# Products with V of query tile 1 issued in pairs, in the attention of a two-block kernel

## The chip, the cores and the metric

The kernel runs on one core of one Trainium2 chip. The metric is the device time of one execution in microseconds (us), as the median of several runs. Beside it stands one profiled execution, whose span runs from the first to the last instruction that the profiler recorded.

The engines are named as in the profile: PE is TensorE (matmuls), PEld its loading of weights, DVE is VectorE, ACT is ScalarE, POOL is GpSimd, SP is SyncE. L1892 is line 1892 of the kernel.

## The reference, cut to what matters

Two transformer-like blocks are computed for 256 tokens of width 1024. The first block has one projection `h @ w_in` that feeds a gated recurrence (RG-LRU) and a sparse attention with three branches: compressed keys, selected blocks of keys, and a window. With 256 tokens the selected blocks and the window both cover every key that the causal mask allows, so both branches are causal attention, each with its own K and V. The change touches the last line of this sum only in the order in which its terms are added:

```python
o_cmp = jnp.einsum('bgrqc,bgcd->bgrqd', p_cmp, v_cmp)
...
o_slc = jnp.einsum('bgrqm,bgqmd->bgrqd', p, vg)
...
o_win = jnp.einsum('bgrqk,bgkd->bgrqd', pw, vwb)
return gb[..., 0:1] * o_cmp + gb[..., 1:2] * o_slc + gb[..., 2:3] * o_win
```

There are 16 query heads in 4 groups of 4; a group shares its keys and values. After it come the output projections, a feed-forward part, and the second block.

## The kernel before

**Chunks.** All weights are streamed in the order of a list, `CHUNKS`. A chunk is up to 128x2048 numbers. For most chunks ACT rounds the weights to a high part `WH` (L629), DVE subtracts to get the low part `WL` (L1074), and PE multiplies both with the activations (L1735, L1736 and L1740 in this stretch of the kernel; a chunk of kind `rnn` has 126 columns, one of kind `mg` 128). Chunks of kind `ri` are not split; PE takes them at L2065, L2073 and L2075.

**Windows.** From chunk `W0` on, chunk W0+w is also window w. PE's program is one loop over the chunks: first the scores of a unit (if one is due), then the chunk itself, then `window(w)`.

**Units.** The attention over selected blocks and window is cut into 12 units, u = 0 to 11, three for each head group g. u%3 = 0 is query tile 0 (queries 0 to 127) with both branches at once; u%3 = 1 is query tile 1 with the first branch, and u%3 = 2 is query tile 1 with the second. A unit goes through these steps, and `UNIT_WINDOWS` says in which window w its scores stand:

- window w, ahead of the chunk: PE computes the scores, `unit_qk` (L1858). It waits for `exp_done`, that is until ACT has read the scores of unit u-1, since there is one place for scores, banks 2 and 3 of PSUM.
- DVE adds the mask (L1095) and finds the maxima (L1097), ACT takes the exponentials (`unit_exp`, L650) into `SM`, or `SMC` where u%3 = 1, and DVE multiplies by gate and reciprocal of the sum (L1112).
- window w+2, behind the chunk: PE transposes the weights, `unit_t` (L1869); ACT (L662) and DVE (L1119) copy the result to `PT`, which has two buffers, `PT[:, u % 2]`. The copy for unit u waits for `pv_done` of unit u-2, which read the same buffer.
- window w+3, behind the chunk: PE multiplies with V, `unit_pv`. For u%3 = 0 and 1 it first starts a sum in bank 6 or 7 with the compressed branch (L1884). Then come four matmuls (L1892), 64 output rows each, in alternating halves of the array. The sum of query tile 1 is left open by u%3 = 1 and closed by u%3 = 2.
- after u%3 = 0 and 2, ACT and DVE copy the sum out of the bank (`o_first` L668, `o_second` L1168) to `CHL`, which the output projection reads.

The windows of the units' scores are 5, 7, 9, 10, 11, 12, 14, 15, 16, 17, 19 and 20. The kinds of the chunks of windows 9 to 24 are mg, rnn, rnn, mg, ri, mg, rnn, rnn, mg, ri, rnn, rnn, mg, mg, ri, ao.

ACT and DVE have fixed programs too, each a loop over the chunks. In them, beside the units, stand the splits of the weights, the reading of the chunks' results, and the recurrence (ACT L717 to L727, with three loads of activation tables of 1.28 us around the square root and the gelu).

In the profile one f32 matmul of `unit_qk` or `unit_pv` counts as two instructions, so a unit's four at L1892 stand as x8.

Of the kernel before, what the change touches and what calls it, by code (L numbers as in the profile page):

```python
# [189 lines left out]
def unit_of(u):  # L190

    g, n = divmod(u, 3)
    return g, int(n > 0), max(n - 1, 0)


def unit_at(w):

    return UNIT_WINDOWS.index(w) if w in UNIT_WINDOWS else None
# [46 lines left out]
def two_block_program(nc, A_w, A_x, A_cols, A_consts, A_g1, A_g2, A_og, A_gln, A_ln1, A_ln2, A_ws, A_out):  # L245
    ctx = ExitStack()
    with ctx:
# [41 lines left out]
        def col(name, j=0, n=1, parts=P):  # L289
            lo = COLS[name][0] + j  # L290
            return CV[0:parts, lo:lo + n]
# [1422 lines left out]
        def _(eng):  # L1714
# [147 lines left out]
            def unit_t(u):  # L1862
                eng.wait_ge(p_ready, u + 1)
                if u >= 1:
                    eng.wait_ge(pt0_copied, u)
                    eng.wait_ge(pt1_copied, u)
                for part in range(2):
                    for i in range(4):
                        last = eng.transpose(PS[:, 4 + part, P * i:P * i + P], sm(u)[:, i, P * part:P * part + P], ident)  # L1869
                last.then_inc(t_done, 1)  # L1870

            def unit_pv(u):
                g, qt, br = unit_of(u)
                v = 2 * g + qt
                bank = 6 + v % 2
                if br == 0:
                    if v == 0:
                        eng.wait_ge(pct_copied, 1)
                        eng.wait_ge(vb_ready, 2)
                    if v >= 2:  # L1880
                        eng.wait_ge(o_lo, v - 1)
                    for pp in range(2):
                        j = 2 * (g % 2) + pp
                        eng.matmul(PS[:, bank, P * pp:P * pp + P],  # L1884
                                   VB[:, g // 2, 2 * j:2 * j + 2, :].rearrange("p h d -> p (h d)"),
                                   PC[:, g // 2, P * qt:P * qt + P], start=(pp == 0), stop=False, skip_group_check=True)
                eng.wait_ge(pt0_copied, u + 1)
                eng.wait_ge(pt1_copied, u + 1)
                for part in range(2):
                    key_tile, branch = (part, br) if qt else (0, part)  # L1890
                    for b in range(2):
                        last = eng.matmul(PS[64 * b:64 * b + 64, bank, 0:256], V[:, key_tile, branch, HD * g:HD * g + HD],  # L1892
                                          PT[:, u % 2, part, 2 * b:2 * b + 2, :].rearrange("p r q -> p (r q)"),
                                          start=False, stop=(part == 1 and (br == 1 or not qt)), skip_group_check=True)
                last.then_inc(pv_done, 1)

            def window(w):
                if w == 0:
                    eng.wait_ge(hg_ready, 2)
                    eng.matmul(PS[:, 3, P:P + NKV * CP], HG[:, 1, :], JJ[:, :], start=True, stop=True).then_inc(hgt_done, 1)  # L1900
                    eng.wait_ge(hk_ready, 1)
                    eng.wait_ge(hk_zero, 1)
                    eng.wait_ge(qkt_copied, 1)
                    eng.matmul(PS[0:NKV * CP, 4, 0:HD], HK[:, 0, :, :].rearrange("p g c -> p (g c)"), col("w2k", n=HD),
                               start=True, stop=True).then_inc(kc_done, 1)
                if w == 1:
                    eng.wait_ge(hvx_ready, 1)
                    eng.wait_ge(hk_zero, 2)
                    eng.wait_ge(qkt_copied, 2)
                    for T in range(2):  # L1910
                        eng.matmul(PS[:, 7, 64 * T:64 * T + 64], HVX[:, 8 * T:8 * T + 8, :].rearrange("p h c -> p (h c)"),
                                   col("w2v", n=HD), start=True, stop=True).then_inc(kc_done, 1)
                if w == 1:
                    eng.wait_ge(knc_ready, 1)
                    eng.transpose(PS[:, 5, 0:NKV * CP], KNC[:, :, :].rearrange("p a d -> p (a d)"),
                                  ident[0:NKV * CP, 0:NKV * CP]).then_inc(kct_done, 1)
                if w == 2:
                    eng.wait_ge(kcz_ready, 1)
                    for j in range(KD):
                        rows = slice(32 * (j % 4), 32 * (j % 4) + 32)  # L1920
                        last = eng.matmul(PS[rows, 5, TOK * (j // 4):TOK * (j // 4) + TOK],
                                          KCZ[:, j // 2, :, :].rearrange("p a c -> p (a c)"), QT[:, j, :], start=True, stop=True)
                    last.then_inc(sc_done, 1)
                    eng.wait_ge(knc_ready, 1)
                    for t in range(NT):
                        last = eng.transpose(PS[:, 4, TOK + 64 * t:TOK + 64 * t + 64], GTT[:, P * t:P * t + P],
                                             ident[0:64, 0:64])
                    last.then_inc(gate_t_done, 1)
                if w == 3:
                    eng.wait_ge(kcz_ready, 2)  # L1930
                    for tt in range(NT):
                        for jj in range(2):
                            o = TOK * tt + P * jj
                            last = eng.transpose(PS[:, 5, o:o + P], SCT[:, TOK * jj + P * tt:TOK * jj + P * tt + P], ident)
                    last.then_inc(sc_done, 1)
                if w == 6:
                    eng.wait_ge(pc_ready, 1)
                    for T in range(2):
                        for tt in range(NT):
                            last = eng.transpose(PS[:, 6, 256 * T + P * tt:256 * T + P * tt + P],  # L1940
                                                 SC[:, tt, 8 * T:8 * T + 8, :].rearrange("p h c -> p (h c)"), ident)
                    last.then_inc(pct_done, 1)
                u = unit_at(w - 2)
                if u is not None:
                    unit_t(u)
                u = unit_at(w - 3)
                if u is not None:
                    unit_pv(u)

            def unit2_qk(u):  # L1950
# [392 lines left out]
            for c in range(NCH):  # L2343
                u = unit_at(c - W0)
                if u is not None:
                    unit_qk(u)
                main(c)
                after(c)
                if c >= W0:
                    window(c - W0)  # L2350
# [170 lines left out]
```

## Time and profile before

| | before |
|---|---|
| median of 3 runs | 812.32 us (812.21 to 812.46) |
| span of the profiled execution | 810.6 us |
| PE busy | 799.6 us (99%) |
| DVE busy | 599.4 us (74%) |
| ACT busy | 487.0 us (60%) |
| mean granted TensorE clock | 0.998 of full |
| DMA | 143.79 MB, mean 177 GB/s |

The profiled execution is 1.7 us shorter by its span than the median run. That is what lies around the span (start and end of the program), and it is taken as the same for both kernels. The units run from about 101 us (first scores) to about 243 us (last product with V).

A row of the timeline gives start, duration, engine, line, operation, tiles, shape and count; in brackets stands the idle time before it and what ended that. Durations overlap, since a matmul starts before the one ahead has drained; what counts on the path is the distance from one start to the next.

### The profile page before, as it was taken

Reading aid. Unit: us, or ns where it says so; the run is one execution under the profiler, and the core shown is the slowest. Engines: PE = TensorE matmul, PEld = TensorE weight load, DVE = VectorE, ACT = ScalarE, POOL = GpSimd, SP = SyncE. Lnnn points to the kernel's source line nnn. Section 1 sums busy time; section 2 is a strip of 40 time slices with the busy share of each in tenths; the row PEclk is TensorE's granted clock in tenths of the full one; section 3 lists DMA queues with packets and bytes.
Section 4 is the critical chain, followed back from the end, with each engine's and each line's share of the span. In section 5 each row is a group of like instructions: output and inputs, shape, how many; then the busy total and the mean of one; then the engine's idle time right before and its main releaser. Section 6 shows DMA issues by size and latency. Waiting matters only on the chain.

```text
span 810.6 us, 11913 instructions
## 1 busy us (share of the span) xinstructions
PE 799.6 (99%) x4813; PEld 693.2 (86%) x4813; DVE 599.4 (74%) x773; ACT 487.0 (60%) x738; POOL 27.1 (3%) x38
## 2 busy tenths in 40 slices
PE   8999999999999999999999999999999999999996
PEld 7889998888888888988888888888888988888885
DVE  6774698998957986897878778877777665655556
ACT  6555598877757454765666566546755654544552
POOL 1102000000000000000000000020110000000000
PEclk9999999999999999999999999999999999999999
DMA  8446432342434674456455555764453655555441
GB/s 337 164 156 251 170 126 104 118 155 73 151 119 159 229 288 156 156 188 227 160 206 174 201 197 175 256 237 147 146 196 121 211 201 196 174 219 191 161 152 52
DMA packets 22630, 143.79 MB, mean 177 GB/s; under 512 B 2608, under 2 KB 3248, under 8 KB 8240
## 3 DMA queue, kind: packets, MB, share of 16 engines
q1 hardware_dynamic: 20880, 137.72, 48.3%
q10 hardware_dynamic: 1696, 5.31, 1.8%
q8 instruction: 38, 0.62, 0.3%
q14 instruction: 16, 0.13, 0.0%
HBM read 141.97 MB, written 1.05 MB: 176 GB/s over the span
## 4 chain that ended last, share of the span: by engine, by line
PE 93%; ACT 3%; DVE 2%; DMA 1%; issue 1%; DVEq 0%; SPq 0%; ACTq 0%
PE PS L1748 19%; PE PS L1752 10%; PE PS L1801 10%; PE PS L1802 10%; PE PS L1805 10%; PE PS L1735 5%; PE PS L1736 4%; PE PS L1740 4%; PE PS L2115 3%; PE PS L1764 2%; PE PS L2094 2%; PE PS L1858 1%; PE PS L1892 1%; PE PS L2119 1%; PE PS L1869 1%; PE PS L2065 1%
## 5 line engine op out<-in xcount | busy, mean ns | idle before, releaser
L1074 DVE TENSOR_TENSOR WL<-RAW,WH 128x2048 fp32r<-128x2048 f32 (+2 forms) x127 | 285.1, 2247 | 31.1 <-ACT WH L629 31.0
L629 ACT ACTIVATE WH<-RAW 128x2048 fp32r<-128x2048 f32 (+2 forms) x127 | 238.2, 1877 | 47.0 <-PE PS L1805 25.7
L1490 DVE TENSOR_TENSOR HLS<-PS,HLS 128x512 f32<-128x512 f32 x46 | 31.7, 689 | 92.7 <-ACT HLS L977 92.7
L1748 PE MATMUL PS<-CHL,WH 128*128 128x512 f32 x352 | 87.9, 392 | 0.0
L1735 PE MATMUL PS<-BHL,WH 128*126 128x256 f32 (+1 forms) x336 | 83.6, 287 | 0.0
L977 ACT ACTIVATE HLS<-PS 128x512 f32<-128x512 f32 x46 | 27.4, 595 | 90.7 <-PE PS L1752 86.3
L1736 PE MATMUL PS<-BHL,WH 128*126 128x256 f32 (+1 forms) x336 | 81.8, 282 | 0.0
L1748 PE MATMUL PS<-BHL,WH 128*128 128x512 f32 x320 | 79.9, 392 | 0.0
L1748 PEld LDWEIGHTS PS<-CHL,WH 128*128 128x128 f32 x352 | 63.9, 189 | 11.8
L1802 PE MATMUL PS<-WH,AHL 128*128 128x512 f32 x176 | 68.8, 391 | 0.0
L1801 PE MATMUL PS<-WH,AHL 128*128 128x512 f32 x176 | 68.7, 390 | 0.0
L1735 PEld LDWEIGHTS PS<-BHL,WH 128*126 128x126 f32 (+1 forms) x336 | 63.4, 189 | 4.6 <-issue 3.7
L1748 PEld LDWEIGHTS PS<-BHL,WH 128*128 128x128 f32 x320 | 58.1, 189 | 10.7
L1736 PEld LDWEIGHTS PS<-BHL,WH 128*126 128x126 f32 (+1 forms) x336 | 63.5, 189 | 0.0
L1801 PE MATMUL PS<-WH,BHL 128*128 128x512 f32 x160 | 63.2, 395 | 0.0
L1802 PE MATMUL PS<-WH,BHL 128*128 128x512 f32 x160 | 62.3, 390 | 0.0
L1805 PE MATMUL PS<-WL,AHL 128*128 128x512 f32 x176 | 54.4, 390 | 0.0
L1752 PEld LDWEIGHTS PS<-CHL,WL 128*128 128x128 f32 x352 | 48.0, 190 | 3.4
L1752 PE MATMUL PS<-CHL,WL 128*128 128x256 f32 x352 | 49.1, 282 | 0.0
L1740 PE MATMUL PS<-BHL,WL 128*126 128x256 f32 (+1 forms) x336 | 46.7, 281 | 0.0
L1752 PEld LDWEIGHTS PS<-BHL,WL 128*128 128x128 f32 x320 | 43.7, 190 | 3.1
L1501 DVE SCALAR_TENSOR_TENSOR CG<-HLS,CV,CG 128x255 f32<-128x255 f32 (+1 forms) x96 | 44.2, 481 | 1.7
(313 smaller groups left out, 1311.1 us busy)
## 6 DMA issues: line engine op xcount, KB each, us to landing
RAW<-in_w_stream SPq DMA_DIRECT2D x108, 1024.0 KB, 4.8
RAW<-in_w_stream SPq DMA_DIRECT2D x11, 1008.0 KB, 4.9
RAW<-in_w_stream SPq DMA_DIRECT2D x8, 704.0 KB, 4.5
WF<-in_w_stream SPq DMA_DIRECT2D x2, 1024.0 KB, 5.4
LN<-in_ln ACTq DMA_DIRECT2D x2, 1024.0 KB, 5.2
WF<-in_w_stream SPq DMA_DIRECT2D x4, 294.0 KB, 3.6
X<-in_x SPq DMA_DIRECT2D x2, 512.0 KB, 4.2
RAW<-in_w_stream SPq DMA_DIRECT2D x2, 512.0 KB, 6.8
```

Of the source, the lines that this page charges most:

```text
L629: eng.activation(WH[:, c % NSLOT, 0:CHUNKS[c][2]], raw(c), ACT.Copy).then_inc(w_hi, 1)
L1074: eng.tensor_tensor(WL[:, c % NSLOT, 0:CHUNKS[c][2]], raw(c), f32(WH[:, c % NSLOT, 0:CHUNKS[c][2]]), ALU.subtract).then_inc(w_lo, 1)
L1490: eng.tensor_tensor(HLS[:, n % 4, :, :], PS[:, bank:bank + 2, 0:TOK], HLS[:, n % 4, :, :], ALU.add)\
L1501: ins = eng.scalar_tensor_tensor(o, HLS[:, i % 4, v, 0:TOK - s], col("fw", (2 - s) * 2 * N_UP + f), o, ALU.mult, ALU.add)
L1735: eng.matmul(out, wh, H[0:parts, k, :], start=(k == 0), stop=False)
L1736: eng.matmul(out, wh, L[0:parts, k, :], start=False, stop=False)
L1740: last = eng.matmul(out, wl, H[0:parts, k, :], start=False, stop=(k == nk - 1))
L1748: eng.matmul(PS[:, bank, :], wh, HL[:, k, :, :].rearrange("p a t -> p (a t)"), start=(k == 0), stop=False)
L1752: last = eng.matmul(PS[:, bank, 0:TOK], wl, HL[:, k, 0, :], start=False, stop=(k == KD - 1))
L1801: eng.matmul(out, H[:, k, tile], wh, start=(start and n == 0), stop=False)
L1802: eng.matmul(out, L[:, k, tile], wh, start=False, stop=False)
L1805: last = eng.matmul(out, H[:, k, tile], WL[:, s, lo_:lo_ + cols], start=False, stop=(stop and n == len(ks) - 1))
```

## The change

Behind the transposes of a window, the kernel before issues the products with V of one unit. The new one leaves them out where u%3 = 1, and issues them one unit later, directly ahead of those of u%3 = 2.

```diff
                 u = unit_at(w - 3)
-                if u is not None:
+                if u is not None and u % 3 != 1:
+                    if u % 3 == 2:
+                        unit_pv(u - 1)
                     unit_pv(u)
```

So `unit_pv(1)` moves from the end of window 10 to the end of window 12, `unit_pv(4)` from 14 to 15, `unit_pv(7)` from 18 to 19, and `unit_pv(10)` from 22 to 23. The order of the units among each other stays, and with it the counts of `pv_done`. ACT's, DVE's, POOL's and SP's instructions stand in the same order as before. Nothing is added or removed.

PE around units 1 and 2, before: the end of window 10 (chunk `rnn`), window 11 with unit 2's transposes at its end, and the end of window 12 with unit 3's. L1858 are the scores of units 4 and 5, L2065 is the `ri` chunk of window 13.

```order
L1740 MATMUL PS<-BHL,WL 126x256 x8
L1884 MATMUL PS<-PC,VB 128x128 x2
L1892 MATMUL PS<-PT,V 64x256 x4
L1858 MATMUL PS<-KT,QT 128x256 x4
...
L1740 MATMUL PS<-BHL,WL 126x256 x8
L1869 MATMUL PS<-CN,SM 128x128 x8
L1858 MATMUL PS<-KT,QT 128x256 x4
...
L1740 MATMUL PS<-BHL,WL 128x256 x8
L1869 MATMUL PS<-CN,SM 128x128 x8
L1892 MATMUL PS<-PT,V 64x256 x4
L2065 MATMUL PS<-XC,WF 126x256 x4
```

The same place in the new kernel, whose lines from 1950 on stand two higher (L2067 is L2065 of before).

```order
L1740 MATMUL PS<-BHL,WL 126x256 x8
L1858 MATMUL PS<-KT,QT 128x256 x4
...
L1740 MATMUL PS<-BHL,WL 126x256 x8
L1869 MATMUL PS<-CN,SM 128x128 x8
L1858 MATMUL PS<-KT,QT 128x256 x4
...
L1740 MATMUL PS<-BHL,WL 128x256 x8
L1869 MATMUL PS<-CN,SM 128x128 x8
L1884 MATMUL PS<-PC,VB 128x128 x2
L1892 MATMUL PS<-PT,V 64x256 x8
L2067 MATMUL PS<-XC,WF 126x256 x4
```

Unit 1's six matmuls have moved past the scores of units 4 and 5, two chunks and two groups of transposes.

PE around units 4 and 5, before: the end of window 14 (chunk `mg`) with unit 5's transposes, and the end of window 15 (chunk `rnn`). L1858 are the scores of units 7 and 8.

```order
L1869 MATMUL PS<-CN,SM 128x128 x8
L1884 MATMUL PS<-PC,VB 128x128 x2
L1892 MATMUL PS<-PT,V 64x256 x4
L1858 MATMUL PS<-KT,QT 128x256 x4
...
L1740 MATMUL PS<-BHL,WL 126x256 x8
L1892 MATMUL PS<-PT,V 64x256 x4
L1858 MATMUL PS<-KT,QT 128x256 x4
```

The same place in the new kernel.

```order
L1869 MATMUL PS<-CN,SM 128x128 x8
L1858 MATMUL PS<-KT,QT 128x256 x4
...
L1740 MATMUL PS<-BHL,WL 126x256 x8
L1884 MATMUL PS<-PC,VB 128x128 x2
L1892 MATMUL PS<-PT,V 64x256 x8
L1858 MATMUL PS<-KT,QT 128x256 x4
```

Here unit 4's matmuls have moved past one group of scores and one chunk. Units 7 and 10 move likewise past one chunk; unit 10's past an `ri` chunk, and no scores.

## Rows read from the trace of the kernel before

**Rows 1.** The page, part 1: busy time, share of the span, instructions of each engine.
```profile
PE 799.6 (99%) x4813; PEld 693.2 (86%) x4813; DVE 599.4 (74%) x773; ACT 487.0 (60%) x738; POOL 27.1 (3%) x38
```

**Rows 2.** Waits of PE, whole span: line, waited for, us in total, times, longest.
```profile
PE PS L2335 <- ACT XN L1026: 1.4, 1, 1.4
PE PS L2329 <- DVE WARM L1640: 1.1, 1, 1.1
PE PS L1858 <- ACT SMC L650: 0.5, 1, 0.5
PE PS L1764 <- DVE CHL L1480: 0.2, 1, 0.2
```

**Rows 3.** Timeline of PE, windows 10 to 13, around units 1 and 2, and the end of window 9.
```profile
135.13 1.03 PE L1869 MATMUL PS<-CN,SMC 128*128 128x128 f32 x8
136.09 1.13 PE L1858 MATMUL PS<-KT,QT 64*128 64x256 f32 x8
...
142.00 1.10 PE L1740 MATMUL PS<-BHL,WL 128*126 128x256 f32 x8
142.94 0.61 PE L1884 MATMUL PS<-PC,VB 128*128 128x128 f32 x4
144.49 1.13 PE L1858 MATMUL PS<-KT,QT 64*128 64x256 f32 x8
...
151.30 1.04 PE L1869 MATMUL PS<-CN,SM 128*128 128x128 f32 x8
152.86 1.13 PE L1858 MATMUL PS<-KT,QT 64*128 64x256 f32 x8 [0.52 <-ACT SMC L650]
...
159.78 1.04 PE L1869 MATMUL PS<-CN,SM 128*128 128x128 f32 x8
160.75 1.08 PE L1892 MATMUL PS<-PT,V 128*64 128x256 f32 x8
161.76 1.99 PE L2065 MATMUL PS<-XC,WF 126*126 126x256 f32 x8
```

**Rows 4.** The chain that ended last, 136 to 154 us: start, us, what.
```profile
136.16 1.09 PE PS L1858 x8
...
142.71 1.72 ACT WH L629
...
147.42 1.28 ACT L727
...
152.86 1.13 PE PS L1858 x8
```

**Rows 5.** Timeline of PE, unit 2's products with V alone, in narrow slices.
```profile
161.23 0.39 PE L1892 MATMUL PS<-PT,V 128*64 128x256 f32 x2
161.45 0.39 PE L1892 MATMUL PS<-PT,V 128*64 128x256 f32 x2
```

**Rows 6.** Timeline of PE, windows 14 and 15, around units 4 and 5.
```profile
174.14 1.03 PE L1869 MATMUL PS<-CN,SM 128*128 128x128 f32 x8
175.01 0.61 PE L1884 MATMUL PS<-PC,VB 128*128 128x128 f32 x4
175.55 1.08 PE L1892 MATMUL PS<-PT,V 128*64 128x256 f32 x8
176.56 1.14 PE L1858 MATMUL PS<-KT,QT 64*128 64x256 f32 x8
...
182.45 1.10 PE L1740 MATMUL PS<-BHL,WL 128*126 128x256 f32 x8
183.48 1.08 PE L1892 MATMUL PS<-PT,V 128*64 128x256 f32 x8
184.49 1.14 PE L1858 MATMUL PS<-KT,QT 64*128 64x256 f32 x8
```

**Rows 7.** Timeline of ACT, the end of unit 6's exponentials.
```profile
174.50 0.24 ACT L650 ACTIVATION_READ_ACCUMULATOR SM<-PS,nb 128x1 f32 x1
```

**Rows 8.** Stretch 144.50 to 152.86: PE, PEld, DVE, ACT, POOL busy (x), clock, DMA.
```profile
144.50:152.86 8.36, 7.84 (x67) 7.23 (x65) 7.86 (x10) 8.27 (x17) 0.00 (x0) 1.00 0.62 237
```

## The prediction, made blind

> **What bounds the kernel now.** Look first at the busy times [rows 1]: PE is busy for 799.6 of 810.6 us, the next engine for 599.4. Then at what PE waits for [rows 2]: over the whole span 3.2 us, 2.5 of them at the start of the program. Only two waits lie later, 0.5 us for ACT's exponentials in the attention and 0.2 us at L1764. So after its first microseconds the kernel is one stream of PE work. What PE does later ends the kernel later, almost one for one, and little idle time is left that could absorb a delay. The one wait in the stretch of the change is the 0.52 us ahead of unit 5's scores at 152.86 [rows 3]. A reorder can do two things to such a stream: change the distances between neighbours, or open a wait. I take these apart pair by pair, always from the start of one group to the start of the next.
>
> **Pair 1, units 1 and 2, the step that decides.** The scores of unit 5 wait for the exponentials of unit 4. What sets their end? Follow the chain back from 152.86 [rows 4]: ACT's exponentials of unit 4, table loads around the recurrence's square root and gelu, the split of a weight chunk at 142.71, unit 3's exponentials, DVE's maxima, and then PE's scores of unit 3 at 136.16. Between 142.71 and 152.86 the chain stays on ACT, which is busy for 8.27 of the last 8.36 us [rows 8]. All of it hangs on something that PE did at 136, ahead of unit 1's products at 142.94 [rows 3]. Taking these products out therefore does not bring the end of unit 4's exponentials forward. Before, PE filled the time with them and waited 0.52 us; now it arrives earlier and waits longer, and still starts at 152.86. The gain up to there is zero.
>
> How much earlier does it arrive? Before, from the last weights of the chunk (142.00) over L1884 to the scores (144.49) it took 2.49 us [rows 3]. Without the products the nearest step is from such a group to a group in half-array form, 182.45 to 183.48, 1.03 us [rows 6]. That is 1.46 us earlier, and the wait grows from 0.52 to about 2.0 us. (The scores of unit 4 then start at 143.03, after the exponentials of unit 3, whose end the chain puts at 142.71, so nothing is spent there.)
>
> Unit 1's products then have to be paid behind unit 3's transposes, after the wait. Before: 159.78 to 161.76, 1.98 us [rows 3]. After: transposes to L1884 0.87 us (174.14 to 175.01), L1884 to L1892 0.54 us (to 175.55) [rows 6], then two units of L1892 in one go. Alone a unit takes 1.01 us (160.75 to 161.76) [rows 3]. Its matmuls start two by two; the third pair at 161.23, the fourth at 161.45, and the next group 0.31 us after that [rows 3, 5]. Joined, I put four more distances of 0.215 us between the first and the last: 1.01 + 0.86 = 1.87. The sum is 0.87 + 0.54 + 1.87 = 3.28, less 1.98: **+1.30 us**. Bounds: without any gain from joining, 1.01 twice, +1.44.
>
> **Pairs 2 and 3, units 4 and 5, 7 and 8.** Here no wait stands behind the place that is emptied. Pair 2 before [rows 6]: 174.14 to 176.56, 2.42, and 182.45 to 184.49, 2.04; together 4.46 us. After: transposes to scores 0.96 (135.13 to 136.09) and chunk to L1884 0.94 [both rows 3], then 0.54 and 1.87, in all 4.31. That is **-0.15 us**. Does a wait open? Unit 7's scores start 1.46 us earlier, at about 175.10, and need unit 6's exponentials, which end at 174.74 [rows 7]. That leaves 0.36 us. Both sides are pushed back by pair 1: PE by 1.30, and ACT through the `ri` chunk whose results it reads next, by the same amount. I count no wait. Pair 3 has the same shape, again with ACT's exponentials behind it: -0.15. In both, ACT's copy to CHL is released where it was, since PE has the same work ahead of it.
>
> **Pair 4, units 10 and 11.** The products pass an `ri` chunk and no scores. Only the joining counts, 1.01 against 0.86: -0.15; the entry into L1884 behind the `ri` chunk has no weights loaded ahead and I give back 0.05. **-0.1 us.**
>
> **The copies.** The copy of unit 3 to PT waits for the products of unit 1, which now stand behind unit 3's transposes rather than two windows ahead. So ACT starts it about 1.5 us later than at present. ACT is queued there with the copy to CHL, which has to wait for unit 2's products anyway, and that one moves by PE's own 1.3. Who needs PT of unit 3 are the transposes of unit 4, behind the next chunk. I count nothing. The same holds for unit 9 behind unit 7. PSUM banks, DMA queues, POOL and SP are untouched.
>
> **Sum.** 1.30 - 0.15 - 0.15 - 0.1 = +0.9 us on the profiled execution, 810.6 to 811.5. With the same 1.7 us around the span, the median of 812.32 goes to **813.2 us**. With both bounds of the joining (nothing gained: four times 0.15 back, +1.5; or pair 1 helped by unit 4's transposes having less to wait for, 0.3 less) this case reaches from 812.8 to 813.9.
>
> **A rule weighed against the rows.** Rows first: between groups that use the array whole and in halves the distance is longer than within a group: 0.31 us at the end of L1892 against 0.215 inside [rows 3, 5]. The Trainium skill, TensorEngine Tiling (Array Packing), Key Properties, says that a change of tiling mode drains TensorE. It speaks for the change: by it, each pair saves the drains that one visit to half-array form costs. The trace agrees in sign, and the joined distance above is its size here; by that rule alone, without the wait of pair 1, the result would be the first rival.
>
> **Rivals.**
> 1. *The chain moves with PE.* If unit 4's exponentials came earlier when unit 4's scores do (now at 143.0 rather than 144.5), pair 1 would save as the others: -0.15 three times and -0.1, 811.8 us. Against it: the chain passes over PE's 144.49 and stays on ACT [rows 4], and ACT has no idle time to close up [rows 8]. 10%.
> 2. *A second wait opens, slower.* Place: unit 7's scores, in window 15. Mechanism: ACT's exponentials of unit 6 are 0.36 us from being late [rows 7], and decide as soon as ACT falls behind PE by more than that after pair 1, for instance by the later copy of unit 3. Price: at most the 1.46 us by which PE comes early, so 813.2 + 1.5 = 814.7 us. 8%.
> 3. *No change.* The added 1.3 us are absorbed by something that also waits on other engines behind 161 us. The waits that are there to absorb it are 0.2 us [rows 2]; more would have to be hidden in distances that show as busy. 812.3 us, 8%.
> 4. *The clock falls.* The granted clock is 1.00 through a wait of 0.52 us [rows 8]; the new wait is about 2.0 us. If the clock fell from 2.4 to 1.2 GHz for the 7.9 us from 152.86 to 160.75 [rows 3], that stretch would take up to 7.9 us more, 821 us. 4%. The Trainium skill, TensorE: Matmul & The Clock Gate, HAM oscillation, says that waits between groups of matmuls can bring the throttle back; no row here shows a fall, so it has the small chance.
>
> The forecast itself has the remaining 70%.
>
> **How the numbers follow.** A measurement of this kernel can tell about 0.2% from no change, here 810.7 and 813.94 us. Faster than that is no case of mine, and is left with 2%. Slower: rivals 2 and 4, 12%, and 5% for an upper end of the forecast that is set too low: 17%. The rest, 81%, is within 0.2%, though most of it on the slow side. The range that leaves out rivals 2 and 4 and holds the forecast, no change and rival 1 is 811.7 to 814.0.
>
> **What would show it.** In the new trace: PE's wait for ACT ahead of unit 5's scores grows from 0.5 to about 2.0 us, and stays the only new one; unit 5's scores start at the same time as before; from unit 3's transposes to the `ri` chunk it takes 3.3 us; L1892 in groups of 16 takes 1.9 us to the next group; behind pair 1 PE runs 1.3 us late, behind pair 4 0.9 us. What would make it wrong: unit 5's scores starting earlier, a wait at another L1858 or at a chunk's first matmul, or a granted clock below 1.00 behind the wait.

## The result, and the profile after

| | before | changed |
|---|---|---|
| median of 20 runs | 812.32 us (812.12 to 812.59) | 812.89 us (812.64 to 814.58) |
| span of the profiled execution | 810.6 us | 810.9 us |

The ratio, which follows the mean of the times rather than the median (as do the ratios below), is 1.0014, with a 95% interval of 1.0008 to 1.0021: slower by 0.14%, less than the 0.2% named in the prediction, which the upper end of the interval just passes. By the medians it is 0.07%. The forecast was 813.2 us.

The median hides something. Before, all times lie within 0.5 us. The changed kernel's 20 times fall into two groups with nothing between: 11 from 812.64 to 812.91 us (median 812.79) and 9 from 814.21 to 814.58 us (median 814.31). The mean granted clock tells the groups apart as well: 0.997 or 0.998 in the lower one, 0.995 or 0.996 in eight executions of the upper one (the ninth, at 814.58 us, shows 0.947; what that was is open). The profiled execution belongs to the lower group, so its trace is read first.

Part 1 of the page, against [rows 1], and PE's waits over the whole span, against [rows 2] (lines from 1950 on stand two higher than before):

```profile
PE 799.1 (99%) x4813; PEld 693.9 (86%) x4813; DVE 598.9 (74%) x773; ACT 487.0 (60%) x738; POOL 27.1 (3%) x38
```

```profile
PE PS L1858 <- ACT SMC L650: 2.0, 1, 2.0
PE PS L2331 <- DVE WARM L1640: 1.1, 1, 1.1
PE PS L2337 <- ACT XN L1026: 0.9, 1, 0.9
PE PS L1764 <- DVE CHL L1480: 0.2, 1, 0.2
```

No wait was added and one has grown, from 0.5 to 2.0 us. The timeline of PE around units 1 and 2, against [rows 3]:

```profile
141.85 1.10 PE L1740 MATMUL PS<-BHL,WL 128*126 128x256 f32 x8
142.88 1.14 PE L1858 MATMUL PS<-KT,QT 64*128 64x256 f32 x8
...
149.70 1.04 PE L1869 MATMUL PS<-CN,SM 128*128 128x128 f32 x8
152.71 0.49 PE L1858 MATMUL PS<-KT,QT 64*128 64x256 f32 x2 [1.98 <-ACT SMC L650]
...
159.63 1.03 PE L1869 MATMUL PS<-CN,SM 128*128 128x128 f32 x8
160.50 0.61 PE L1884 MATMUL PS<-PC,VB 128*128 128x128 f32 x4
161.04 1.95 PE L1892 MATMUL PS<-PT,V 128*64 128x256 f32 x16
162.92 1.99 PE L2067 MATMUL PS<-XC,WF 126*126 126x256 f32 x8
```

This execution left its first wait for ACT 0.15 us earlier than that of before, and everything up to 142 us stands 0.15 us earlier. With that taken off, unit 5's scores (152.71) start exactly where they did. PE came 1.46 us earlier and waited 1.46 us longer. From unit 3's transposes to the `ri` chunk it now takes 3.29 us, against 1.98. Around units 4 and 5, against [rows 6]:

```profile
175.25 1.04 PE L1869 MATMUL PS<-CN,SM 128*128 128x128 f32 x8
176.21 1.14 PE L1858 MATMUL PS<-KT,QT 64*128 64x256 f32 x8
...
182.12 1.10 PE L1740 MATMUL PS<-BHL,WL 128*126 128x256 f32 x8
183.06 0.61 PE L1884 MATMUL PS<-PC,VB 128*128 128x128 f32 x4
183.59 1.95 PE L1892 MATMUL PS<-PT,V 128*64 128x256 f32 x16
185.47 1.13 PE L1858 MATMUL PS<-KT,QT 64*128 64x256 f32 x8
```

Here the two stretches take 0.96 + 3.35 = 4.31 us against 4.46, and no wait opened. In the table below an `ao` chunk is one of the projection behind the attention (L2094, L2096 in the changed kernel), an `ro` chunk one of that behind the recurrence (L2115 and L2119, L2117 and L2121). How far PE is behind the kernel before, place by place (the 0.15 us of the start added back):

| place | before | changed | PE late by |
|---|---|---|---|
| scores of unit 5 | 152.86 | 152.71 | 0.00 |
| `ri` chunk of window 13 | 161.76 | 162.92 | 1.31 |
| transposes of unit 4 | 164.77 | 165.84 | 1.22 |
| scores of unit 8 | 184.49 | 185.47 | 1.13 |
| scores of unit 11 | 215.86 | 216.67 | 0.96 |
| first `ao` chunk | 243.06 | 243.75 | 0.84 |
| L2119 of the `ro` chunk that starts at 281 us | 283.66 | 284.03 | 0.52 |

The last 0.5 us is what the lower group is slower by, 812.79 against 812.32. Two things are open: where 0.3 us went between 243 and 284 us, and what lifts every other execution by 1.5 us.

### The profile page after: what moved, and what is told of

Its sections match the earlier page's. It is cut to its first block, busy times and chain, and to the rows that moved or that the text cites. A ratio compares the mean times of both kernels' runs of the same rounds, so it can differ in the third digit from the quotient of the medians.

```text
span 810.9 us, 11913 instructions
## 1 busy us (share of the span) xinstructions
PE 799.1 (99%) x4813; PEld 693.9 (86%) x4813; DVE 598.9 (74%) x773; ACT 487.0 (60%) x738; POOL 27.1 (3%) x38
## 4 chain that ended last, share of the span: by engine, by line
PE 93%; ACT 3%; DVE 2%; DMA 1%; issue 0%; DVEq 0%; SPq 0%; ACTq 0%
PE PS L1748 19%; PE PS L1752 10%; PE PS L1801 10%; PE PS L1805 10%; PE PS L1802 10%; PE PS L1735 5%; PE PS L1736 4%; PE PS L1740 4%; PE PS L2117 2%; PE PS L1764 2%; PE PS L2096 2%; PE PS L1858 1%; PE PS L1892 1%; PE PS L2121 1%; PE PS L1869 1%; PE PS L2067 1%
## 5 line engine op out<-in xcount | busy, mean ns | idle before, releaser
L1074 DVE TENSOR_TENSOR WL<-RAW,WH 128x2048 fp32r<-128x2048 f32 (+2 forms) x127 | 284.5, 2242 | 32.1 <-ACT WH L629 32.0
```

The lines of the kernel that those rows point to most:

```text
L1074: eng.tensor_tensor(WL[:, c % NSLOT, 0:CHUNKS[c][2]], raw(c), f32(WH[:, c % NSLOT, 0:CHUNKS[c][2]]), ALU.subtract).then_inc(w_lo, 1)
```

## The experiments

Each was timed beside the kernel before on the same chip, and there are three chips. The first holds pair 1 alone, pairs 2 to 4, unit 1 in the wait and the changed kernel once more (before: 812.35 us). The second holds the waits filled with six and with three matmuls, pair 4 alone, and the wait filled with needed work (before: 812.26 us). The third holds the wait with one matmul and the two kernels with the shorter ACT chain (before: 812.39 us). The changed kernel itself was not timed on the second and third.

**Pair 1 alone, and the other pairs alone.** The condition on u%3 is replaced by units 1 and 2; in the second kernel the lists are (4, 7, 10) and (5, 8, 11).

```diff
-                if u is not None and u % 3 != 1:
-                    if u % 3 == 2:
+                if u is not None and u != 1:
+                    if u == 2:
```

> Only unit 1's products are moved behind unit 3's transposes, next to unit 2's; units 4, 7 and 10 stay where they were. Theory (the time is lost at one wait: unit 5's scores wait for unit 4's exponentials, whose end PE's order does not move): PE's wait ahead of unit 5's scores grows from 0.5 to 2.0 us, and the kernel is 1.2 us slower than before, more than the whole change. Rival (paired products cost a little wherever they are, for instance through the later copy to PT): a quarter of the whole loss, 0.1 to 0.2 us.

Measured: 815.05 us (ratio 1.0026, interval 1.0014 to 1.0037), in two groups again: three of seven times at 813.71 to 813.86, four at 815.05 to 815.21. The lower group is 1.4 us slower than before, where 1.2 was forecast.

> Units 4, 7 and 10 are moved, unit 1's products stay. Theory: no wait opens; three joinings save 0.13 to 0.16 us each, and with the ri chunk ahead of unit 10's products ACT and DVE run 0.8 us earlier at 246 us, which takes away 0.35 us at 281 us: 0.8 us faster than before. Rival (each pair costs alike): 0.3 to 0.5 us slower.

Measured: 811.52 us (811.45 to 811.61, one group), ratio 0.999 (0.9981 to 0.9999), 0.8 us faster. So the loss belongs to pair 1 alone, and the other three pairs gain. The rival, by which each pair costs alike, is out. Added up, the two parts give +0.6 us (1.4 less 0.8), and the lower group of the changed kernel is +0.5.

**Unit 1's products into the wait.**

```diff
+                if w == 11:
+                    unit_pv(1)
                 u = unit_at(w - 3)
                 if u is not None and u % 3 != 1:
-                    if u % 3 == 2:
+                    if u in (5, 8, 11):
                         unit_pv(u - 1)
```

> As the changed kernel, but unit 1's products stand one window earlier, behind unit 2's transposes and ahead of unit 5's scores, where PE waits for ACT. Theory: they fit into the 2.0 us of waiting (about 1.5 us), the wait is back at about 0.5 us, unit 5's scores still start at the same time, and nothing is paid later: 0.8 us faster than before, as with pairs 2 to 4 alone. Rival (the later products as such cost): slower than that by 0.3 us or more.

Measured: 811.53 us (811.36 to 811.77), ratio 0.999 (0.9981 to 0.9999), the same as without any move of unit 1. The timeline of PE shows why: the products stand in the time that PE would have waited, and the next scores still start at 152.72.

```profile
149.73 1.04 PE L1869 MATMUL PS<-CN,SM 128*128 128x128 f32 x8
150.60 0.61 PE L1884 MATMUL PS<-PC,VB 128*128 128x128 f32 x4
151.14 1.08 PE L1892 MATMUL PS<-PT,V 128*64 128x256 f32 x8
152.72 0.70 PE L1858 MATMUL PS<-KT,QT 64*128 64x256 f32 x4 [0.50 <-ACT SMC L650]
```

**The changed kernel once more.**

> The changed kernel once more, as it is, beside the others on one chip. Its first 20 times fell into two groups, 812.6 to 812.9 and 814.2 to 814.6 us. Theory A (the two groups belong to the placement of unit 1's products): they show here and with pair 1 only, and not with pairs 2 to 4. Theory B (they belong to the pairs behind it): they show with pairs 2 to 4. Theory C (chance of that chip): none here.

Measured: 814.20 us (812.55 to 814.38), ratio 1.0017 (1.0008 to 1.0025): four of 11 times in the lower group, seven in the upper. With pair 1 alone both groups are there; with pairs 2 to 4 alone, and with unit 1 in the wait, there is one, on the same chip: theory A. This profiled execution belongs to the upper group (span 812.5 us, mean clock 0.996). By stretches (length, busy time of PE, PEld, DVE, ACT and POOL, granted clock, DMA share, GB/s), first of this execution:

```profile
149.00:152.00 3.00, 1.82 (x17) 1.58 (x15) 2.93 (x5) 2.97 (x7) 0.00 (x0) 1.00 0.62 261
152.00:153.00 1.00, 0.22 (x2) 0.22 (x4) 0.50 (x1) 1.00 (x5) 0.00 (x0) 1.00 0.00 0
153.00:156.00 3.00, 3.00 (x17) 2.34 (x15) 2.37 (x5) 2.74 (x4) 0.00 (x0) 0.58 0.00 0
156.00:159.00 3.00, 3.00 (x23) 3.00 (x23) 2.90 (x5) 1.43 (x7) 0.00 (x0) 0.85 0.02 5
159.00:163.00 4.00, 4.00 (x36) 3.81 (x36) 3.97 (x4) 1.10 (x4) 0.00 (x0) 1.00 0.22 36
```

then of the lower group's:

```profile
153.00:156.00 3.00, 3.00 (x26) 2.62 (x25) 2.44 (x5) 2.68 (x4) 0.00 (x0) 1.00 0.03 5
156.00:159.00 3.00, 3.00 (x27) 3.00 (x26) 2.90 (x6) 1.50 (x7) 0.00 (x0) 1.00 0.00 0
```

The clock is at 1.00 up to and through the wait, and a little beyond it; then TensorE runs at the lower of its two levels, 1.2 GHz (0.50 of full). Narrower stretches place it, first in this execution, then in that of pair 1 alone, which belongs to its kernel's upper group too:

```profile
153.50:156.75 3.25, 3.25 (x16) 2.64 (x15) 3.09 (x6) 2.24 (x2) 0.00 (x0) 0.50 0.02 5
```

```profile
154.40:157.50 3.10, 3.10 (x16) 3.10 (x16) 3.03 (x6) 1.36 (x1) 0.00 (x0) 0.50 0.03 5
```

PE went on at 152.78 in the one and at 152.79 in the other. The clock fell at 153.5 in the one and at 154.3 in the other, 0.7 and 1.5 us later, and stayed down for about 3.4 us in both. The timeline of PE of this execution shows the same in the steps:

```profile
152.78 1.42 PE L1858 MATMUL PS<-KT,QT 64*128 64x256 f32 x8 [1.96 <-ACT SMC L650]
154.12 0.58 PE L1735 MATMUL PS<-BHL,WH 128*128 128x256 f32 x1
154.50 0.42 PE L1736 MATMUL PS<-BHL,WH 128*128 128x256 f32 x1
154.72 0.42 PE L1735 MATMUL PS<-BHL,WH 128*128 128x256 f32 x1
...
156.85 0.32 PE L1735 MATMUL PS<-BHL,WH 128*128 128x256 f32 x1
157.01 0.28 PE L1736 MATMUL PS<-BHL,WH 128*128 128x256 f32 x1
157.13 0.28 PE L1735 MATMUL PS<-BHL,WH 128*128 128x256 f32 x1
```

From start to start it is 0.21 to 0.22 us from 154.50 up to 156.85 and 0.12 us from 157.01 on. At 156.85 PE stands 1.5 us behind the same matmul of the lower group's execution (155.31), which is the distance between the groups. The clock goes with the group in every execution taken, of whichever kernel: all 21 in an upper group have a mean granted clock of 0.996 or less, all others one of 0.997 to 0.999.

**Is it the length of the standstill?** The changed kernel gets work that nobody needs, where PE waits; n is 6, 3 or 1.

```diff
+                if w == 11:
+                    for _ in range(n):
+                        eng.matmul(PS[:, 7, 3 * P:4 * P], ident, ident, start=True, stop=True, skip_group_check=True)
```

> As the changed kernel, with six matmuls of 128 columns of the identity behind unit 2's transposes, where PE waits about 2.0 us for unit 4's exponentials; their result goes to columns of bank 7 that nobody reads. It is work that nobody needs, put only where PE stands still. Theory (the upper group of times, 1.5 us above the lower, is the clock that falls to half behind the 2.0 us wait): with the wait cut to 0.5 to 1.0 us only the lower group is left, about 812.8 us, with the clock at 1.00 behind the wait. Rival (the upper group belongs to the order itself): two groups as before, near 812.8 and 814.3 us.

Measured: 812.72 us (812.62 to 813.19), ratio 1.0006 (0.9997 to 1.0015). The wait is 0.6 us, and no time is in the upper group; one, 813.19 us, stands above the others, with a mean clock of 0.998.

> The same with three such matmuls, so that the wait is cut about in half, to 1.2 to 1.6 us. Theory: the shorter PE stands still, the fewer executions fall to half clock; between 0 and a third of the times in the upper group, against about half in the changed kernel. Rival (any wait of over 1 us will do): about half, as in the changed kernel.

Measured: 812.73 us (812.60 to 812.94), ratio 1.0006 (0.9997 to 1.0015). The wait is 1.3 us, none of 11 times in the upper group.

> As the run with three matmuls of the identity in the wait, but with one, so that about 1.7 to 1.75 us of waiting are left. The upper group of times was seen in about half of the executions with a wait of 2.0 us and in none of 11 with 1.3 us. Theory (its share grows with the length of the standstill): between a tenth and a half of the times here. Rival (any activity between 149 and 153 us is enough): none.

Measured: 812.78 us (812.70 to 814.43), ratio 1.0007 (0.9998 to 1.0016). The wait is 1.8 us, one of 11 times in the upper group, at the lower end of what was expected. The order of all needed work is that of the changed kernel in each of the three, so the order alone does not make the upper group. With a shorter standstill, be it filled with useless work, it is rare or absent. One reservation stays: these three ran on the second and third chip, where the changed kernel was not timed, and how often a wait of 2.0 us drops the clock there is not known. On the first chip it is 11 of 18 with a wait of 2.0 us against none of 51 with 0.5 us.

| wait ahead of unit 5's scores | kernels | times in the upper group |
|---|---|---|
| 0.0 to 0.6 us | before, pairs 2 to 4, pair 4 alone, unit 1 in the wait, n = 6, the wait filled with needed work, before with the shorter ACT chain | 0 of 175 |
| 1.3 us | n = 3, and the changed kernel with the shorter ACT chain below | 0 of 22 |
| 1.8 us | n = 1 | 1 of 11 |
| 2.0 us | changed (twice), pair 1 alone | 20 of 38 |

**What sets the wait?** In the changed kernel, and in the second one below in the kernel before, ACT copies instead of taking the gelu of the recurrence's second group, which leaves out one load of activation tables; the output is then another.

```diff
-                    eng.activation(RGT[:, G % 2, 0:n, :], RGT[:, G % 2, 0:n, :], ACT.Gelu_apprx_tanh)\
+                    eng.activation(RGT[:, G % 2, 0:n, :], RGT[:, G % 2, 0:n, :], ACT.Copy if G == 1 else ACT.Gelu_apprx_tanh)\
```

> The changed kernel, in which ACT copies instead of taking the gelu of the recurrence's second group (L727, in window 10), so that the output is another; this leaves out one load of activation tables, 1.28 us, from ACT's chain between units 3 and 4. Theory (the wait ahead of unit 5's scores is set by ACT's chain alone): the wait shrinks from 2.0 to about 0.7 us, the lower group of times goes from 812.7 to 811.4 us, and the upper group is gone. Rival (the wait is set by PE's own order): no change beyond 0.2 us.

Measured: 812.06 us (811.98 to 812.21, one group), ratio 0.9996 (0.9987 to 1.0005). The wait went from 2.0 to 1.3 us, not to 0.7, and the time to 812.1, not to 811.4. The timeline of ACT shows what came late next:

```profile
147.41 0.83 ACT L727 ACTIVATE RGT<-RGT 126x768 f32<-126x768 f32 x1
148.26 1.28 ACT L650 ACT_TABLE_LOAD   x1
150.27 0.47 ACT L650 ACTIVATE SMC<-PS,nb 128x256 f32<-128x256 f32 x1 [0.73 <-DVE nb L1097]
```

ACT was ready 1.3 us sooner and then waited 0.73 us for DVE's maxima. Two chains run side by side to these exponentials, and DVE's is only some 0.6 us (1.3 less 0.7) shorter. The change of PE's order moved neither: DVE's maxima start at 148.91 us before and at 148.76 in the changed kernel, which is the 0.15 us of the start.

> The same left out of the kernel before. Theory: only its 0.52 us of waiting can be won, 811.8 us; with the run above, the changed kernel is then the faster of the two by 0.3 to 0.5 us, while it is 0.5 us slower with the longer ACT chain. Rival: 1.3 us won, as in the run above.

Measured: 811.66 us (811.59 to 811.81), ratio 0.9991 (0.9982 to 1.0). It won 0.7 us, all its 0.5 us of waiting, and about 0.2 us more, whose source was not looked into; its unit 5's scores start 0.6 us earlier (152.20 in a trace that started 0.07 us earlier) with no wait ahead. The prediction that the changed kernel would overtake it failed, since the changed one still waits 1.3 us for exponentials that DVE's maxima now hold up: it is 0.4 us slower than this one.

**Pair 4 alone**: the condition names u = 10 and 11 only.

> Only unit 10's products are moved, behind the ri chunk and next to unit 11's. Theory (the ri chunk that goes ahead sets ACT and DVE 0.8 to 1.5 us earlier at 246 us and so takes away PE's 0.35 us at 281 us, besides 0.15 us of joining): 0.5 us faster than before, 811.8 us, and the distance from L2119 to L2115 at 281 us is as short as its neighbours. Rival (only the joining counts): 0.1 to 0.15 us faster.

Measured: 811.79 us (811.62 to 811.99), ratio 0.9993 (0.9984 to 1.0002), 0.47 us faster by the medians. The interval just holds no change, but all 11 times lie below the lowest of the kernel before (812.06), and the trace shows where the time went. First the kernel before, then this one, timeline of PE around 281 us:

```profile
275.65 1.48 PE L2119 MATMUL PS<-AHL,WL 126*128 126x256 f32 x11
276.96 2.68 PE L2115 MATMUL PS<-AHL,WH 126*128 126x512 f32 x11
279.48 1.47 PE L2119 MATMUL PS<-AHL,WL 126*128 126x256 f32 x11
281.06 2.76 PE L2115 MATMUL PS<-AHL,WH 126*128 126x512 f32 x11
283.66 1.48 PE L2119 MATMUL PS<-AHL,WL 126*128 126x256 f32 x11
```

```profile
276.86 2.68 PE L2117 MATMUL PS<-AHL,WH 126*128 126x512 f32 x11
279.38 1.48 PE L2121 MATMUL PS<-AHL,WL 126*128 126x256 f32 x11
280.69 2.68 PE L2117 MATMUL PS<-AHL,WH 126*128 126x512 f32 x11
283.21 1.48 PE L2121 MATMUL PS<-AHL,WL 126*128 126x256 f32 x11
```

Before, one distance is 1.58 us where its neighbour is 1.31, and the next 2.60 where the other is 2.52: 0.35 us that no view calls a wait. With the `ri` chunk ahead of unit 10's products both are gone. The kernel says what the first was: from the fifth `ro` chunk on, which is the one at 281 us, PE waits for `m_ready` (L2111), here for DVE's third L1322. Before, then with pair 4 alone:

```profile
280.49 0.42 DVE L1322 TENSOR_TENSOR MG<-MG,RS 128x256 f32<-128x256 f32 x1
```

```profile
279.01 0.42 DVE L1322 TENSOR_TENSOR MG<-MG,RS 128x256 f32<-128x256 f32 x1
```

Before, it ends at 280.91 us, and PE, which could have gone on at 280.79 (1.31 us after 279.48), starts at 281.06, 0.27 us late. (The other 0.08 us is the first matmul of that group, which takes 0.47 us where the others take 0.39.) With pair 4 alone it ends at 279.43, well ahead of PE's 280.69. Why DVE is earlier stands upstream. ACT reads the `ri` chunk's results, then splits a weight chunk, and only then copies unit 11's sum for DVE. DVE before and in the changed kernel:

```profile
245.88 0.42 DVE L1168 TENSOR_TENSOR CHL<-PS,CHL 128x256 fp32r<-128x256 f32 x1 [6.21 <-ACT CHL L668]
```

```profile
245.07 0.42 DVE L1168 TENSOR_TENSOR CHL<-PS,CHL 128x256 fp32r<-128x256 f32 x1 [4.55 <-ACT CHL L668]
```

In the changed kernel DVE goes on 0.8 us earlier although PE is 0.8 us behind, and its next splits of weights (L1074) keep that lead, 0.81 to 0.86 us, up to the one at 283.70 us (284.56 before).

**The wait filled with needed work.** Unit 1's products and the compressed part of unit 3's sum both stand behind unit 2's transposes; pairs 2 to 4 as in the changed kernel. `compressed(3)` is the two matmuls of L1884 for unit 3 (L1883 in this kernel), which `unit_pv(3)` then leaves out.

```diff
 ...
+                if w == 11:
+                    unit_pv(1)
+                    compressed(3)
 ...
```

> Pairs 2 to 4 as in the changed kernel; behind unit 2's transposes, where PE waits, stand unit 1's products and also the compressed part of unit 3's sum (L1884, two matmuls in bank 6, 0.54 us), which then isn't issued with unit 3. Theory (what stands in the wait costs nothing and is saved later): the 0.5 us of wait that the earlier run had left are used up, and it is 0.4 to 0.5 us faster than that run, 811.1 us. Rival (the wait is set by PE's own arrival): no faster than 811.5 us.

Measured: 811.25 us (811.16 to 811.50), ratio 0.9987 (0.9979 to 0.9996), about 1.0 us faster than before and the fastest of all. PE has no wait left there: the second group of compressed products runs up to the scores. They start at 152.88 us, against 152.72 with unit 1 alone in the wait, and 0.09 us of that is a later start of this trace, already there ahead of the wait (150.69 against 150.60).

```profile
152.24 0.71 PE L1883 MATMUL PS<-PC,VB 128*128 128x128 f32 x4
152.88 0.70 PE L1858 MATMUL PS<-KT,QT 64*128 64x256 f32 x4
```

By the medians it gained 0.2 us over the earlier kernel (1.01 us against 0.82 us, each beside its own runs of before; the two intervals overlap), not the 0.4 to 0.5 us expected. Against that kernel's trace, unit 6's scores start at 166.74 and not at 167.09, and unit 10's at 205.12 and not at 205.33. With the 0.09 us of the start added, that is 0.44 and 0.30 us earlier. So the saving was there behind unit 3, in the size expected, and part of it was lost before 205 us; to what was not looked into.

## Why the prediction was right, point by point

**Pair 1.** Right in mechanism and size: +1.30 forecast, 1.31 in the trace. The wait grew by the 1.46 us named. (The upper bound without joining is 1.45 by its own terms, not 1.44.) Filling it cost nothing and leaving the move out saved the loss, so it is the placement across this wait that costs. That ACT alone sets the wait was too simple: DVE's chain to the same exponentials is some 0.6 us behind, and the run with a shorter ACT chain showed it.

**The joining.** Right: sixteen L1892 take 1.88 us to the next group (1.87 forecast). Pair 2 came out at -0.15, as forecast. The place table gives 0.09 to 0.17 us for each pair, with neighbouring effects of 0.04 to 0.09 us mixed in. The first of these is at unit 4's transposes, 0.09 us less behind the `ri` chunk, which the prediction only named as a bound: before, they start at 164.77 us, just behind DVE's copy of unit 3 (L1119, 163.94 to 164.62), and in the changed kernel that copy is long done. The longer distance behind the last L1892, 0.31 us against 0.215 within the group, is some 0.1 us for each visit. By the Trainium skill's TensorEngine Tiling (Array Packing), Key Properties, a change of tiling mode drains the array. The trace agrees in sign; that the drain is the whole of this distance was not tested.

**The copies.** Right: ACT's copy of unit 3 to PT starts at 162.24 us and not at 160.85, 1.5 us later with the start taken off, the copy to CHL 1.3 us later, and no wait of PE came of it.

**Pair 4.** Mis-sized. Up to the first `ao` chunk it is -0.12 us in the place table, as the -0.1 forecast. (The 0.05 us that the prediction gave back rests on no row; behind the `ri` chunk L1884 takes 0.64 us to L1892, 241.23 to 241.87, against 0.54 elsewhere.) But with what it sets free at 281 us it is about -0.5 us alone. The step that failed is "Only the joining counts". The `ri` chunk that goes ahead hands its results to ACT 0.8 us earlier, and DVE, behind ACT, then has L1322 done in time for the `ro` chunk 40 us later, where PE had lost 0.35 us. This is most of the difference between 813.2 and the lower group's 812.8.

**The range of the case.** Its ends were given as 812.8 and 813.9; by the prediction's own terms they are 812.9 (813.2 less 0.3) and 813.8 (812.32 and 1.5).

**No second wait (rival 2), no help from the chain (rival 1).** Right: the waits of PE show neither.

**The clock (rival 4).** This had 4% and came in about every other execution. Its price was put at up to 7.9 us, for the whole stretch; it was 1.5 us, since the clock came back after about 3.4 us. The reason for the low chance was that no row showed a fall after a wait; but no row showed a wait of 2.0 us in a running stream either. The rule of the Trainium skill, TensorE: Matmul & The Clock Gate, HAM oscillation, that waiting between groups of matmuls can bring the throttle back, is borne out, and here by a single wait of 2.0 us. Of the 31 times taken of the changed kernel, 16 are in the upper group. All of them, at 814.2 us and more, lie above the range that was given (814.0), and so does the median of the second 11 (814.20).

So the number was right partly by chance: it left out 0.3 us of gain at 281 us and a loss of 1.5 us in every second execution, and the median of the 20 times happened to fall into the lower group, by 11 to 9.

## What to carry to other kernels

In a kernel that one engine bounds, moving its work past a place where it waits for another engine costs nearly the work's whole time (here 1.30 of 1.46 us): the wait swallows the gain, and the work is paid behind it. Look for the wait first and put into it what is ready, rather than taking out what fills it. And look at all the times, not the median alone: a kernel can have two. Last, ask of a wait that no view shows (here 0.27 us at 281 us) which semaphore the code waits for at that line, and when the other engine gave it.

## What the runs showed of the hardware

After a single wait of 2.0 us in an otherwise dense stream of matmuls, TensorE's granted clock fell from 2.4 to 1.2 GHz in 20 of 38 executions, at a cost of 1.5 us. In the two of them whose traces are kept it fell not at once but 0.7 and 1.5 us after the matmuls had gone on, and stayed down for about 3.4 us. With waits of 1.8 us it did so in 1 of 11, with 1.3 us in none of 22, with 0.6 us or less in none of 175; the 1.8 and 1.3 us were measured on other chips than the repeated runs with 2.0 us. Whether it falls differs between executions of one kernel on one chip; what decides it was not tested.
